# The first attention head's preparation in an MLA layer: head 0's k, rope and q products ahead of the second gate unit, the second gate's activation moved into head 0, and the PSUM banks dealt out anew

## The reference

```python
def _mla_mixer(x, pos, w_in, q_norm, w_q_up, kv_norm, w_kv_up, w_out):
    h = x @ w_in
    c_q, c_kv, k_rope, g = jnp.split(h, [Q_LORA, Q_LORA + KV_LORA, Q_LORA + KV_LORA + QK_ROPE], axis=-1)
    q = (_rms_norm(c_q, q_norm) @ w_q_up).reshape(B, L, H, QK_NOPE + QK_ROPE)
    q_nope, q_rope = q[..., :QK_NOPE], _rope(q[..., QK_NOPE:], pos)
    kv = (_rms_norm(c_kv, kv_norm) @ w_kv_up).reshape(B, L, H, QK_NOPE + V_HEAD)
    k_nope, v = kv[..., :QK_NOPE], kv[..., QK_NOPE:]
    k_rope = _rope(k_rope, pos)
    o = _causal_block_attention(q_nope, q_rope, k_nope, k_rope, v).reshape(B, L, D_INNER)
    return (o * jax.nn.silu(g)) @ w_out
```

## Time and profile before

| | |
|---|---|
| median of 3 runs | 2340.19 us (2339.62 to 2341.67) |
| the profiled execution | 2341.81 us |
| its span in the trace | 2340.1 us |
| share of the span that PE was busy | 98% |
| share of DVE, POOL, ACT | 52%, 49%, 36% |
| mean granted TensorE clock | 0.993 of full |
| the MLA heads in the trace | from 1894.52 us on |

### The profile page before, as it was taken

How to read it: one execution, slowest core, us unless ns; L and a number is a source line. 1 busy time by engine, 2 the same in 40 slices (tenths; PEclk the granted TensorE clock), 3 DMA queues, 4 the chain that set the end, 5 groups by cost and what they waited for, 6 DMA issues and landing times.

```text
span 2340.1 us, 51380 instructions
## 1 busy us (share of the span) xinstructions
PE 2284.0 (98%) x21811; PEld 1778.8 (76%) x21811; DVE 1213.5 (52%) x2312; ACT 852.8 (36%) x1765; POOL 1151.3 (49%) x771
## 2 busy tenths in 40 slices
PE   8999999999999999999999999999998999999998
PEld 7788887888887667777777777777887877877776
DVE  4353268877804655555555555555421565555511
ACT  4122212333302455555555555555320343443400
POOL 4555566788763434443444433334455344344345
PEclk9999999999999999999999999999999999999999
DMA  3333233333322322222222222223322322121212
GB/s 113 82 82 81 80 92 90 97 93 99 110 99 65 94 61 72 67 67 67 67 67 67 71 72 67 67 67 130 121 87 85 105 67 55 47 61 46 99 64 90
DMA packets 262109, 188.04 MB, mean 80 GB/s; under 512 B 18284, under 2 KB 242410, under 8 KB 261498
## 3 DMA queue, kind: packets, MB, share of 16 engines
q1 hardware_dynamic: 261881, 184.76, 26.3%
HBM read 162.69 MB, written 22.04 MB: 79 GB/s over the span
## 4 chain that ended last, share of the span: by engine, by line
PE 91%; DVE 5%; POOL 1%; issue 1%; DMA 0%; SPq 0%; ACT 0%; POOLq 0%; DVEq 0%; ACTq 0%
PE ps L1354 19%; PE ps L159 16%; PE ps L160 15%; PE ps L161 15%; PE ps L1529 3%; PE ps L1545 3%; PE ps L1571 2%; PE ps L1484 2%; PE ps L2450 2%; PE ps L1456 2%; PE ps L1518 2%; PE ps L1367 1%; PE ps L221 1%; PE ps L1475 1%; PE ps L1501 1%
## 5 line engine op out<-in xcount | busy, mean ns | idle before, releaser
L150 POOL TENSOR_TENSOR w_lo<-raw,w_hi 128x1024 fp32r<-128x1024 f32 (+1 forms) x178 | 453.6, 2549 | 14.8
L147 POOL TENSOR_SCALAR w_hi<-raw 128x1024 fp32r<-128x1024 f32 (+1 forms) x178 | 196.4, 1104 | 501.6 <-PE ps L161 490.8
L159 PE MATMUL ps<-h_hi,w_hi 128*128 128x512 f32 x616 | 243.1, 395 | 1.8 <-DVE h_lo L1062 1.7
L161 PE MATMUL ps<-h_hi,w_lo 128*128 128x512 f32 x616 | 240.1, 390 | 0.0
L160 PE MATMUL ps<-h_lo,w_hi 128*128 128x512 f32 x616 | 239.8, 389 | 0.0
L1932 POOL TENSOR_TENSOR kp<-k_b,kp 128x528 f32<-128x528 f32 x16 | 29.5, 1845 | 350.8 <-ACT kp L1668 350.8
L1354 PE MATMUL ps<-mixed_r,raw 128*64 128x264 f32 x1024 | 152.7, 387 | 0.0
L1354 PE MATMUL ps<-mixed_k,raw 128*64 128x264 f32 x1024 | 138.3, 389 | 0.0
L159 PEld LDWEIGHTS ps<-h_hi,w_hi 128*128 128x128 f32 x616 | 115.9, 188 | 26.2 <-DVE h_lo L1062 2.8
L161 PEld LDWEIGHTS ps<-h_hi,w_lo 128*128 128x128 f32 x616 | 115.6, 188 | 24.5
L160 PEld LDWEIGHTS ps<-h_lo,w_hi 128*128 128x128 f32 x616 | 115.8, 188 | 23.1
(11 more groups left out here) (452 smaller groups left out, 5834.3 us busy)
## 6 DMA issues: line engine op xcount, KB each, us to landing
raw<-in_rwkv_w_in_dram SPq DMA_DIRECT2D x64, 512.0 KB, 4.1
raw<-in_w_up_dram SPq DMA_DIRECT2D x44, 512.0 KB, 3.8
raw<-in_w_in_dram SPq DMA_DIRECT2D x41, 512.0 KB, 3.9
raw<-in_w_down_dram SPq DMA_DIRECT2D x22, 512.0 KB, 3.6
raw<-in_mla_w_in_dram SPq DMA_DIRECT2D x22, 512.0 KB, 4.1
sb_kept<-xT SPq DMA_DIRECT2D x16, 528.0 KB, 2.7
xT<-sb_kept SPq DMA_DIRECT2D x16, 528.0 KB, 4.2
raw<-in_rwkv_w_out_dram SPq DMA_DIRECT2D x16, 512.0 KB, 4.3
```

Of the source, the lines that this page charges most:

```text
L147: nc.gpsimd.tensor_scalar(w_hi[s][:, 0:width], raw[s][:, 0:width], 1.0, 0.0, ALU.mult, ALU.add).then_inc(split_hi, 1)
L150: nc.gpsimd.tensor_tensor(w_lo[s][:, 0:width], raw[s][:, 0:width], w_hi[s][:, 0:width].bitcast(F32), ALU.subtract).then_inc(split_ready, 1)
L159: nc.tensor.matmul(dst, w[0], x[0], start=start, stop=False)
L161: return nc.tensor.matmul(dst, w[1], x[0], start=False, stop=stop)
```

## The change

Five edits, all in the MLA layer:

- `MLA_UNITS`: unit A of pair 0 comes second, gate 1's third. SP's loads and POOL's splits follow this list.
- `FILLS`: gate 0, ka, rope, qn, kb, gate 1 in place of gate 0, gate 1, rope, ka, qn, kb, and the first six banks are 6, 4, 5, 6, 7, 4 in place of 6, 4, 5, 6, 4, 5.
- DVE: gate 0's output goes ahead of the three instructions of `k_rot`, ka's low part between them and the parts of the rope key, and gate 1's output behind the last of the rope queries' parts, as the last instruction ahead of the heads.
- ACT: ka's output goes ahead of rope's. Gate 1's silu is taken out of the part ahead of the heads and stands in head 0, behind the exp of block 1.
- `head_act`: the condition `and h` goes, by which head 0 had no silu.

The core of the diff:

```diff
-        MLA_UNITS = [("gate", 0), ("gate", 1), ("A", 0)]
+        MLA_UNITS = [("gate", 0), ("A", 0), ("gate", 1)]
...
-        FILLS = [("gate", 0), ("gate", 1), ("rope", 0), ("ka", 0), ("qn", 0), ("kb", 0)]
+        FILLS = [("gate", 0), ("ka", 0), ("rope", 0), ("qn", 0), ("kb", 0), ("gate", 1)]
...
-        FILL_BANK = [6, 4, 5, 6, 4, 5] + [BANK_OF[kind] for kind, _ in FILLS[6:]]
+        FILL_BANK = [6, 4, 5, 6, 7, 4] + [BANK_OF[kind] for kind, _ in FILLS[6:]]
...
-                if t == 1 and h and h + AHEAD <= MH:
+                if t == 1 and h + AHEAD <= MH:
                     gate_silu(act, h + AHEAD - 1)
...
-                for g in range(2):
-                    gate_silu(act, g)
-                for n in range(2, 6):
-                    fill_out(act, FILLS[n])
+                gate_silu(act, 0)
+                for item in FILLS[1:5]:
+                    fill_out(act, item)
...
+                gate_out(dve, 0)
                 dve.wait_ge(k_step, 2)
...
-                for g in range(2):
-                    gate_out(dve, g)
+                low_out(dve, ("ka", 0))
...
-                for item in FILLS[3:6]:
+                for item in FILLS[3:5]:
                     low_out(dve, item)
                 rope_parts(dve, 1)
+                gate_out(dve, 1)
```

## The result

The changed kernel takes 2345.97 us in the median of 10 runs (2343.98 to 2348.1), the kernel before 2340.11 in 10 runs beside it (2339.25 to 2341.67). The ratio is 1.0025, 95% interval 1.0017 to 1.0033: slower by 5.9 us. I had forecast 2341.7, no change, and a range up to 2344.2.

A forecast was written before the change was run, and what follows sets the result against it. PE's own work was taken as the bound (91% of the chain), with one 3.45 us hole; −0.2 − 1.0 + 2.5 − 0.5 = +0.8, plus +0.7 for low clock, gave +1.5 us: 2341.7 on the median, range 2337.4 to 2344.2.

The forecast's parts named there:

- A's split earlier: POOL's split from 1871.33 takes 1280 columns instead of 1024, so L239 of c_kv and the norm come 0.77 us later.
- The last ckv_lo: End of the c_kv norm on DVE: falls behind POOL's next split, waits for w_hi, ends near 1880.4 instead of 1878.87.
- PE ahead of ka: After gate 0, PE idles 2.1 us waiting for the c_kv norm; without the lock 0.5 us.
- DVE up to the scores: Unit B's split holds DVE's low part of the rope queries; head 0's scores start at 1894.35, −0.2 us.
- my sign of being wrong: Among the signs listed against the forecast: L2389 of head 1's rope queries on DVE taking 0.7 us.
- Clock of the scores: Head 0's scores of blocks 0 and 1 run at full clock, 1.45 us in place of 2.49: −1.0 us.
- v0 waits anew: After head 0's scores, v0 waits for its bank until gate_out(1), held behind L2389 and gate 2's split: +2.5 us.
- v0, v1 and the low clock: v0 and v1 at full clock, 2.9 us for 3.41: −0.5; low clock behind the new hole, half of 1.5: +0.7.
- the rival that ends on the other side: Slower by over 0.2%: low clock after several idle times; with a third low stretch +5.5 us, 2345.7; chance 0.06.
- ACT in head 0: Gate 1's silu and two table loads, 3.2 us, fit in head 0 with 1.8 us spare: no cost.
- the shift stays to the end: Behind turn 0, head 0 and later heads keep their lists with PE busy, so the +1.5 us carries through unchanged.
- it gains as meant: Rival: DVE gets ahead of POOL's splits before the scores and v0; turn 0 −2.9 us, 2337.3; chance 0.2.

The follow-up runs named there:

- e7: Changed kernel with two waits in POOL's list: gate 1's split waits for the last ckv_lo, unit B's split for kb's low part on DVE; 2337.9 us.
- e4: Changed kernel with 8, 5 and 10 matmuls that nothing reads put into PE's three holes, ahead of ka, the scores and v0; 2341.81 us.
- e1: Changed kernel with gate 1's output moved ahead of head 1's rope query parts in DVE's list; 2341.94 us.
- e2: Changed kernel with kb in bank 4 and gate 1 in bank 7, DVE's list unchanged; 2340.82 us.
- e5: Kernel before, with only gate 1's silu and its two table loads moved into head 0, behind exp 1; 2340.81 us.
- e6: Kernel before, with 13 matmuls that nothing reads ahead of head 0's first scores; 2338.0 us.
- e10: Changed kernel with rope ahead of ka in the fills, ACT's and DVE's lists, and gate 1 in bank 5; POOL's list as changed; 2337.73 us.
- e12: Changed kernel with rope ahead of ka, gate 1 in bank 5, and POOL's splits of gate 1 and unit B waiting for DVE; 2337.43 us.
- e8: Changed kernel with POOL's splits of gate 1 and unit B waiting for DVE, plus kb in bank 4 and gate 1 in bank 7; 2338.19 us.
- e9: Changed kernel with only unit B's split on POOL waiting for kb's low part on DVE; 2339.27 us.
- e11: Kernel before, with only unit B's split on POOL waiting for kb's low part on DVE; 2342.15 us.

## Why the prediction was wrong

The direction of the shift and its places were right, its size was not. By its own steps:

1. *A's split earlier*: right. L239 took 2.19, the norm came 0.77 later against gate 0's start.
2. *The last ckv_lo*: right. It lost the race, 1.42 us in place of 0.71. Gate 0's output behind it (L2350, from 1879.42) took 0.68 us, all of it beside POOL's w_lo of 1879.03, so an instruction that reads PSUM is not held; my two in the earlier trace rows had run beside POOL in part only, from 1884.26.
3. *PE ahead of ka*: right, 2.11 us for 2.1. Without the lost race it is 1.40 (e7); my 0.5 had left out the 0.77 of step 1.
4. *DVE up to the scores*: the mechanism was right, a rope part waited for unit B's w_lo. Not −0.2: counted from gate 0's first matmul, the scores start 1.8 us later than before (23.84 against 22.05). Most of ka and half of rope ran at the low clock behind the first hole, so rope's read-out and the end of kb, behind which unit B's split starts, were late. This I had not put into the sum; without low clock (e4) the scores start at 22.25, so 1.6 of it is that. And both times the cast (L2387) was held, not the low part (L2389) that I had named. By the letter my sign of being wrong, L2389 of head 1 at 0.7 us, has come (0.69), since the cast ahead of it had taken the wait.
5. *Clock of the scores*: right, full, from 1895.45. But the stretch in which their hole lies was itself followed by the low clock, from 1897.1.
6. *v0 waits anew*: right, 2.56 us for 2.5, and released by gate_out(1). e1 and e2 show it from two sides.
7. and 8. *v0, v1 and the low clock*: **this is the term that was mis-sized.** I gave the clock +0.7 against a gain of 1.5 at the scores and in v0 and v1. It cost 3.5 in the stage by e4. The hole ahead of ka got a low stretch, for which the forecast had nothing. Two more came on end: the first began as the hole ahead of v0 did, behind the hole ahead of the scores, the second behind the one ahead of v0. V0 and v1 took 4.86 us, where I had 2.9. I had named this as the rival that ends on the other side, three low stretches and +5.5, and gave it 0.06. The row that I cited spoke against an even chance: behind PE busy 1.75 of 3.40 us the clock had fallen, and I applied that to one hole of three.
9. *ACT in head 0*: right for this kernel, in which ACT holds up nothing, and e5 shows no cost. It was luck in part: the late v0 hid the 0.8 us that e1 and e2 wait at v2.

The sum over the stage: holes +2.7 (forecast 2.25), clock +1.9 against before (3.5 less the 1.6 that e6 takes from the kernel before; forecast −0.8), together 4.6 of the 4.9 measured. The step "the shift stays to the end" missed the rest: 1.75 us came in the last heads, where one more low stretch fell in this execution. The profiled execution had more low clock than most: its granted clock over the whole span is 0.991, as in two others of the ten, and these three are the slowest (2347.19 to 2348.1 us); the seven others have 0.992 (2343.98 to 2346.18). Where in the program those had less was not recorded, so how the last microsecond of the 5.9 in the medians divides stays open, and so does whether the change has to do with that second stretch.

Of the rivals, "it gains as meant" held as a mechanism: with the races taken away (e7) the same order is faster than before, by 2.1 us (0.9991, 0.9983 to 1.0), where I had worked out 2.9.

## What to carry to other kernels

A PE wait of 2 us or more had two prices here, itself and the clock that followed, and waits of 1.3 to 1.7 us had the second in some kernels only; where several small holes replace one larger, ask for the low clock behind each, and count what the slow work holds up behind it. When work is moved to fill a hole, look at what the moved work had covered (here the c_kv norm), at who shares its bank, and at what stands ahead of its read-out in the other engine's list. And where POOL and DVE alternate on SBUF, the start of POOL's long instruction is a part of the schedule: two waits that only delayed it were worth 8.1 us here (e7), as much as the best order of PE's fills with its banks (e10, 8.2), and the two together hardly more (e12, 8.5).

## What the runs showed of the hardware

- The low clock followed a stretch with PE busy 1.87 of 3.40 us, with the work on both sides of one hole of 1.49 us (the row from 1893.70). I had taken a hole of 2.5 us as an even chance. The length of a hole alone did not tell: waits of 1.28 to 1.54 us in e1, e2, e7, e8, e9 and e12 had no low stretch behind them, one of 1.72 in e10 had, and so had each of 2.1 us or more that was not filled.
- Two low stretches on end came where a second hole fell into the first of them (the changed kernel and e11).
- Matmuls that nothing reads paid where they fitted the hole: 13 of them made the kernel before 2.0 us faster in the medians (e6, 0.9989), 23 the changed kernel 4.2 us (e4).
- A DVE cast of 0.42 us takes 3.07 beside POOL's subtraction and ends 0.3 behind it, a two-input instruction 0.56 behind it (L2858 and L2864 in the earlier trace rows); the delay came and went with the start of POOL's instruction (e7). The Trainium skill (SBUF — State Buffer, section "Who interferes with whom") says the same in the sentence that issue order decides who blocks; e7 and e9 agree, with 8.1 and 6.7 us against the changed kernel.
